# A two-layer decoder with a mixture of experts: expert weights in 16 KB runs, the first expert's rows gathered, the routing lists computed in one piece

## The reference, cut to what matters

```python
h = rms_norm(x, ffn_norm[layer])                  # 512 x 1024
grp_p = softmax(h @ w_group + b_group)            # 4 groups, the best one is taken
top_p, top_i = top_k(softmax(logits of that group), 2)   # 2 of its 4 experts
combine[token, expert] = weight of that expert for that token (0 for the other 14)
for e in range(16):
    act = silu(h @ w_gate[e]) * (h @ w_up[e])     # w_gate, w_up: 1024 x 512
    y = y + combine[:, e:e + 1] * (act @ w_down[e])      # w_down: 512 x 1024
x = x + y
```

## Time and profile before

| | us |
|---|---|
| median of 3 runs (lowest, highest) | 1287.82 (1285.38, 1289.57) |
| the profiled execution: its time | 1285.25 |
| the profiled execution: its span | 1283.5 |
| TensorE busy in the span | 1180.3 (92%) |
| VectorE busy | 914.7 (71%) |
| ScalarE busy | 674.1 (53%) |
| DMA, mean over the span | 220 GB/s |
| the two MoE parts | about 340 to 665 and 944 to 1283.5 |

### The profile page before, as it was taken

The page is one execution under the profiler, slowest core; times in us unless marked ns, Lnnn a source line. Parts: engine busy times, 40 slices in busy tenths (PEclk is TensorE's granted clock), DMA queues, the critical chain, the costliest instruction groups (busy, mean ns, idle before and its releaser), DMA issues.

```text
span 1283.5 us, 16959 instructions
## 1 busy us (share of the span) xinstructions
PE 1180.3 (92%) x5788; PEld 898.5 (70%) x5788; DVE 914.7 (71%) x1251; ACT 674.1 (53%) x843; POOL 97.3 (8%) x128
## 2 busy tenths in 40 slices
PE   5999879999799999999878999999979999999986
PEld 4776669878776766766646688887876666667663
DVE  4646668656579888888967247646558898888886
ACT  4335651134347778777733242132426777787862
POOL 1120000000010000000030000001001100000003
PEclk9999999999899999999989999999979999999998
DMA  6231110123599999999860240113169999999955
GB/s 221 91 89 66 66 66 1 66 73 125 187 331 363 366 385 390 384 382 384 332 220 1 70 136 15 66 66 131 66 257 303 368 381 381 383 391 385 381 203 209
DMA packets 129423, 281.75 MB, mean 220 GB/s; under 512 B 18945, under 2 KB 19457, under 8 KB 129361
## 3 DMA queue, kind: packets, MB, share of 16 engines
q1 hardware_dynamic: 119680, 246.98, 53.2%
q0 software_dynamic: 5888, 20.97, 5.3%
q10 hardware_dynamic: 3792, 12.98, 2.7%
HBM read 262.05 MB, written 18.87 MB: 219 GB/s over the span
## 4 chain that ended last, share of the span: by engine, by line
PE 57%; DVE 25%; issue 9%; ACT 6%; POOL 1%; DMA 1%; DVEq 1%; ACTq 0%; SPq 0%
PE PS L1109 16%; PE PS L1111 15%; PE PS L1110 15%; DVE expert_w_low L1824 10%; PE PS L1213 4%; DVE group_low L1612 2%; PE PS L1343 2%; ACT weight_high L870 1%; PE PS L1148 1%; DVE xgT_low L1832 1%; DVE act L1845 1%; DVE score_max L1743 1%; DVE G L1502 1%; PE PS L1323 1%; DVE hT_low L1596 1%
## 5 line engine op out<-in xcount | busy, mean ns | idle before, releaser
L1824 DVE TENSOR_TENSOR expert_w_low<-expert_w,weight_high 128x1024 fp32r<-128x1024 f32 x368 | 426.5, 1221 | 75.0 <-ACT weight_high L870 71.3
L870 ACT ACTIVATE weight_high<-expert_w 128x1024 fp32r<-128x1024 f32 x384 | 375.5, 1049 | 69.6 <-PE PS L1111 61.9
L1109 PE MATMUL PS<-weight_high,xgT_high 128*96 128x512 f32 x512 | 204.5, 399 | 2.6 <-DVEq L1834 2.6
L1111 PE MATMUL PS<-weight_high,xgT_low 128*96 128x512 f32 x512 | 203.2, 397 | 0.0
L1110 PE MATMUL PS<-expert_w_low,xgT_high 128*96 128x512 f32 x512 | 202.1, 395 | 0.0
L1109 PE MATMUL PS<-group_high,hT_high 128*128 128x512 f32 x416 | 172.2, 414 | 13.9 <-DVEq L1599 9.5
L1111 PE MATMUL PS<-group_high,hT_low 128*128 128x512 f32 x416 | 165.3, 397 | 0.0
L1110 PE MATMUL PS<-group_low,hT_high 128*128 128x512 f32 x416 | 165.0, 397 | 0.0
L1109 PE MATMUL PS<-weight_high,actT_high 128*96 128x512 f32 x256 | 104.3, 407 | 19.4 <-DVEq L1882 18.9
L1612 DVE TENSOR_TENSOR group_low<-group_w,group_high 128x1024 fp32r<-128x1024 f32 x68 | 80.8, 1223 | 43.4 <-ACT group_high L894 39.5
L1109 PEld LDWEIGHTS PS<-weight_high,xgT_high 128*96 128x96 f32 x512 | 83.3, 163 | 36.0 <-DVEq L1834 2.7
(11 more groups left out here) (251 smaller groups left out, 1469.9 us busy)
## 6 DMA issues: line engine op xcount, KB each, us to landing
expert_w<-in_moe_w_gate SPq DMA_DIRECT2D x32, 2048.0 KB, 13.7
expert_w<-in_moe_w_up SPq DMA_DIRECT2D x32, 2048.0 KB, 15.0
expert_w<-in_moe_w_down SPq DMA_DIRECT2D x32, 2048.0 KB, 13.5
group_w<-in_even_w_in SPq DMA_DIRECT2D x6, 2048.0 KB, 7.8
group_w<-in_odd_w_in SPq DMA_DIRECT2D x6, 2048.0 KB, 8.1
y_rows<-yb ACTq DMA_DIRECT2D x30, 384.0 KB, 6.1
group_w<-in_even_w_out SPq DMA_DIRECT2D x2, 2048.0 KB, 7.9
h_rows<-h SPq DMA_DIRECT2D x8, 512.0 KB, 11.3
```

Source lines behind the costliest of these rows:

```text
L870: act_(hi, w, ACT.Copy).then_inc(w_hi, 1)
L1109: pe.matmul(out, ah, bh, start=first, stop=False)
L1111: return pe.matmul(out, al, bh, start=False, stop=final)
L1824: tt(lo, w, hi.bitcast(F32), ALU.subtract).then_inc(w_lo, 1)
```

## The change

1. The weight view becomes `(p k) n -> p (a k) n`: partition p takes rows 8p to 8p+7 (gate, up) or 4p to 4p+3 (down), one run of 16 KB. To match, `h` ahead of the MoE is written with its columns in the order k, j from j*8+k, and `act` from j*4+k. VectorE does both by reading its two inputs with a step of 8 or of 4 elements; the output is written in order. The mixers' weights keep their view.
2. `oh0` and its 64 matmuls go. The rows of expert 0 are gathered like the others: the first indirect DMA takes column 0 of `idx`, the loop gathers 1 to 15, and TensorE transposes block 0's rows with `rows_T(0)`. SP no longer waits for the matmuls before it loads gate of expert 2.
3. VectorE's order at the start changes: after the one-hots `ohj` come two pieces of `first_low(1)`, `idx`, the other two pieces, the tokens' weights, the last expert's one-hots, the overflow counts, `b` and `j`, the instructions of `slots`, then the low part of block 0's rows, the instructions of `further`, the low part of block 1's rows, all of gate of expert 1, `times_up(0)`. ScalarE: rows 0, rows 1, the last one-hots' copy, high part of gate, then `silu(0)`. TensorE: gate 0, `rows_T(1)`, the last one-hots' transposes, up 0.

```diff
-                    src = t["moe_w_" + name][l, bass.ds(e, 1)].rearrange("a (k p) n -> p (a k) n", p=P)
+                    src = t["moe_w_" + name][l, bass.ds(e, 1)].rearrange("a (p k) n -> p (a k) n", p=P)
...
                 sp.wait_ge(h_stored, 16 * NT * (l + 1))
                 bk.wait_full(sp, ("route", l))
-                bk.wait_full(sp, ("xgT", l))
                 expert("gate", 2, 5)
...
-                pool.indirect_dma_start(xg[0:CAP, :], None, hbuf[l][:], bass.IndirectOffsetOnAxis(idx[:, 1:2], 0)
+                pool.indirect_dma_start(xg[0:CAP, :], None, hbuf[l][:], bass.IndirectOffsetOnAxis(idx[:, 0:1], 0)
                                         ).then_inc(gathered, 16)
-                with pool.Fori(2, NE) as b:
+                with pool.Fori(1, NE) as b:
...
                 rows_T(0, 0)
-                silu(0)
-                high(GATE, which=range(0, 2))
                 rows_T(1, 1)
-                high(GATE, which=range(2, SPLITS))
                 key = ("lastT", l)
                 bk.wait_full(sc, key)
                 link(act_(lastT[:], bank(key)[0:CAP], ACT.Copy))
                 sc.sem_inc(bk.freed(key), 1)
+                bk.wait_full(sc, ("gate", l))
+                high(GATE)
+                silu(0)
...
-                key = ("xgT", l)
-                pe.wait_ge(h_ready, NT * (2 * l + 2))
-                pe.wait_ge(oh0_ready, l + 1)
-                bk.acquire_in_loop(pe, key, 0)
-                for c in range(KD):
-                    for i in range(NT):
-                        ins = pe.matmul(PS[:, 4 + c // 4, c % 4 * CAP:(c % 4 + 1) * CAP], h[:, i, c * P:(c + 1) * P],
-                                        oh0[:, i], start=i == 0, stop=i == NT - 1)
-                ins.then_inc(bk.filled(key), 1)
...
+                rows_T(0)
                 pe.wait_ge(xgT_ready, l * NE + 1)
                 into("gate", 0, 0, 0, 0, 0)
-                into("up", 0, 0, 1, 0, 0, lambda: rows_T(1))
+                rows_T(1)
                 key = ("lastT", l)
...
+                into("up", 0, 0, 1, 0, 0)
                 expert_loop(pe, block_pe)
...
+            act_parts = act[0:CAP].rearrange("p (k j) -> p k j", k=DE // P)
+            def in_parts_of(a):
+                return a.rearrange("p (j k) -> p k j", k=DE // P)
...
-                        stt(h[:, i], x[:, i], xrs[:, i:i + 1], normw[:], ALU.mult, ALU.mult).then_inc(h_ready, 1)
+                        dst, xi, nw = h[:, i], x[:, i], normw[:]
+                        if n % 2:
+                            dst = dst.rearrange("p (k j) -> p k j", k=KD)
+                            xi, nw = (a.rearrange("p (j k) -> p k j", k=KD) for a in (xi, nw))
+                        stt(dst, xi, xrs[:, i:i + 1], nw, ALU.mult, ALU.mult).then_inc(h_ready, 1)
...
-                for i in range(NT):
-                    ins = ts(oh0[:, i], iota_f[:, 0:CAP], rank[:, i, 0:1], r["M"][:, i, 0:1], ALU.is_equal, ALU.mult)
-                link(ins)
-                ve.sem_inc(oh0_ready, 1)
...
+                first_low(1, range(0, 2))
+                key = ("idx", l)
+                bk.wait_full(ve, key)
+                link(cp(idx[:, 0:NE], bank(key)[0:CAP, 0:NE]))
+                ve.sem_inc(idx_ready, 1)
+                ve.sem_inc(bk.freed(key), 1)
+                first_low(1, range(2, SPLITS))
...
-                    link(tt(act[0:CAP], bank(("up", l))[0:CAP], ex[0:CAP], ALU.mult))
+                    link(tt(act_parts, in_parts_of(bank(("up", l))[0:CAP]), in_parts_of(ex[0:CAP]), ALU.mult))
...
-                    if is_int and b == 0:
-                        slots()
-                    if is_int and b == NE - 3:
-                        further()
```

More of the change, by code:

```diff
@@ L368, in build @@
         ).items():
-            if name == "ein":
-                oh0 = at("first_onehot", [P, NT, CAP], F32, cursor[0])
             rt[name] = sb("r_" + name, [P] + shape)
@@ L418, in build @@
         idxcol_ready, gathered = sem("idxcol_ready"), sem("gathered")
-        oh0_ready = sem("first_onehot_ready")
         xgT_ready, ex_ready = sem("xgT_ready"), sem("gate_silu_ready")
@@ L798, in _ @@
                 pool.sem_inc(gather_issued, 1)
-                pool.indirect_dma_start(xg[0:CAP, :], None, hbuf[l][:], bass.IndirectOffsetOnAxis(idx[:, 1:2], 0)
+                pool.indirect_dma_start(xg[0:CAP, :], None, hbuf[l][:], bass.IndirectOffsetOnAxis(idx[:, 0:1], 0)
                                         ).then_inc(gathered, 16)
-                with pool.Fori(2, NE) as b:
+                with pool.Fori(1, NE) as b:
                     bk.wait_full(pool, ("xgT", l), b - 1)
-                    gather(l, b, idxcol_ready, b + (l * (NE - 2) - 1), gathered)
+                    gather(l, b, idxcol_ready, b + l * (NE - 1), gathered)
                 pool.wait_ge(eid_ready, l + 1)
@@ L864, in _, with high @@
             for l in range(NL):
-                def high(p0, b=0, par=0, which=range(SPLITS)):
+                def high(p0, b=0, par=0):
                     wait_loaded(sc, l, p0, b, par)
-                    for part in which:
+                    for part in range(SPLITS):
                         w, hi, _ = parts(l, p0, par, part)
@@ L1364, in rows_T @@
                     key = ("xgT", l)
-                    pe.wait_ge(gathered, b * 16 + 16 * l * (NE - 1))
+                    pe.wait_ge(gathered, b * 16 + 16 * (l * NE + 1))
                     bk.acquire_in_loop(pe, key, b)
@@ L1908, in _ @@
                 link(tt(r["w_last"], r["w_of"][:, 0], r["w_of"][:, 1], ALU.add))
+                for i in range(NT):
+                    ins = ts(ohj[:, i], iota_f[:, 0:CAP], rank[:, i, NE - 1:NE], r["M"][:, i, NE - 1:NE], ALU.is_equal, ALU.mult)
+                link(ins)
+                ve.sem_inc(last_ready, 1)
                 link(ts(r["nx"], total, float(CAP), None, ALU.is_gt))
@@ L1913, in _ @@
                 link(tt(r["off"], r["off"], r["nx"], ALU.subtract))
[L1914 to L1920, removed]
                 link(ts(r["q"], rank, float(CAP), None, ALU.is_ge))
@@ L1930, in _ @@
                 link(stt(r["j"], r["q"], -float(CAP), rank, ALU.mult, ALU.add))
[L1931 to L1936, removed]
+                for of, by in (("bc", "b"), ("jc", "j")):
+                    link(tt(r["tA"], r["OH"], r[by].unsqueeze(1).broadcast_to(both), ALU.mult))
+                    link(red(r[of], r["tA"], AX, ALU.add))
+                link(stt(r["jz"], r["bc"], float(NE - 1), r["jc"], ALU.not_equal, ALU.mult))
+                link(stt(r["sl"], r["bc"], float(CAP), r["jz"], ALU.mult, ALU.add))
+                link(cp(slot[:], r["sl"]))
+                rows_T(0, 0)
+                it8 = iota_f[:, 0:16].unsqueeze(2).broadcast_to([P, 16, NE])
+                off8 = r["off"].unsqueeze(1).broadcast_to([P, 16, NE])
+                nx8 = r["nx"].unsqueeze(1).broadcast_to([P, 16, NE])
+                link(tt(r["ein"], it8, off8, ALU.subtract))
+                link(tt(r["ein2"], r["ein"], nx8, ALU.is_lt))
+                link(stt(r["ein2"], r["ein"], 0.0, r["ein2"], ALU.is_ge, ALU.mult))
+                link(tt(r["ein2"], r["ein2"], iota_f[:, 0:NE].unsqueeze(1).broadcast_to([P, 16, NE]), ALU.mult))
+                link(red(r["eidf"], r["ein2"], AX, ALU.add))
+                link(red(r["eidf"][:, 15:16], r["nx"], AX, ALU.add))
+                link(cp(eid[:], r["eidf"]))
+                ve.sem_inc(eid_ready, 1)
                 rows_T(1, 1)
-                low(GATE, which=range(2, SPLITS))
+                low(GATE)
                 times_up(0)
@@ L1952, in _ @@
                         ve.wait_ge(ov_pe[l], b * 4 + 3)
-                        tt(act[0:CAP], PS[0:CAP, 1, :], ex[0:CAP], ALU.mult).then_inc(ov_ve[l], 1)
+                        tt(act_parts, in_parts_of(PS[0:CAP, 1, :]), in_parts_of(ex[0:CAP]), ALU.mult).then_inc(ov_ve[l], 1)
             for kind, i in sums[NL - 1]:
```

## The result

The changed kernel took **1304.78 us** (median of 3 runs, 1303.42 to 1305.05) against 1287.82: slower by 1.3%, ratio 1.0131 with a 95% interval of 1.0102 to 1.0159. The forecast was 1292.3 with a range to 1301. Its profiled span is 1301.7 us against 1283.5, so 18.2 us are to be found.

What follows compares the result with a forecast made beforehand. TensorE's matmuls were taken to bound the blocks, VectorE right behind. Per layer 3.3 + 0.74 + 3.8 + 0.5 + 0.4 - 1.6 - 4.9 = +2.2 us, twice +4.5: 1292.3 us on the median, 8-in-10 range 1283.5 to 1301.

Steps and rivals of the forecast that it cites:

- The start: From `r_R` to the first gate matmul: 17.75 us instead of 13.96, set by VectorE's list, +3.8 us a layer.
- the gather comes late: Rival at the start: gather rows wait behind 16 KB runs, +4.2 to +6 us in all, 1296.5 to 1298.3; chance 0.10.
- Stepped reads: VectorE's `act` and `h`: 0.72 ns an element, 0.37 us per `act` on 9 of 16 blocks, 0.74 us for `h`.
- Both rivals on the steps: At `act` and `h`: steps cost nothing, 1284.2 us, chance 0.22; or two stepped inputs add up, 1300.4 us, chance 0.18.
- the lower bound of 0: VectorE's stepped reads: least extra cost 0, since L1692's second level, step of 2, takes the plain 693 ns.
- The runs themselves: Expert weight loads in 16 KB runs: 0 us, since nothing waits for a load.
- Block 0: ScalarE's `silu(0)` and table load after high part of gate delay VectorE's low of down: +0.4 us a layer, bounds 0 and +0.9.
- What goes: `slots` out of block 1, -1.6 us; `further` out of block 14 with its low clock, -4.9 us together, a layer.
- The clock: Low clock around 640 us goes, saving 1.7 us; gate matmuls at the start run low 4 us instead of 3, +0.5.

Runs made afterwards that it cites:

- the lists moved alone: Kernel before with b, j and slots moved into VectorE's pause beside the one-hot matmuls and further taking the place of b and j: 1275.43 us, ratio 0.9896.

## Why the prediction was wrong

**The start: this step failed.** "So the gather hides with 0.4 us to spare" took the median landing of 7.2 us from the old blocks. The parts beside it were right, or nearly: `idx` at 4.72, the issue at 5.86 (forecast 5.87), the list done at 16.1; only the handover behind it was 0.11 us instead of 0.66, so the list alone gives a start of 17.2 (measured with all loads held) and not 17.75. The gather was at the edge even with short runs: 8.0 us to TensorE in L0, 8.8 in L1, where it ended the start. In the changed kernel it took 12.2 and 11.8 us, so the start took 21.65 and 21.18 instead of 17.75: 7.3 us over the forecast in all. The rival "the gather comes late" named the place and the mechanism, 6 rows an engine each behind a 16 KB run, which is what the packet counts show, but had 0.10 and was priced by the worst landing of the old runs. I argued against it that the blocks show 7.2 "under the same load"; that row was measured with 2 and 4 KB runs, which the change takes away. And SP's earlier load of gate of expert 2 was booked at 0 "as nobody waits for it". Holding it back gives 7.3 us: it put nobody off but the gather, which by then TensorE waits for.

**Stepped reads: right.** +0.39 us an `act` against 0.37: runs and steps alone cost 3.0 and 3.5 us a layer between first gate matmul and the last `act`, 8 and 9 times 0.39 (forecast 3.3 for 9), 8.7 in all (forecast for `act` and `h` 8.1). `h` costs 0.91 against 0.74. Both rivals on the steps fall. The figure of 2.50 ns a column by the Trainium skill, page "Vector Engine (DVE) Microarchitecture Reference", section "Measured stream behaviour on trn2", is for a longer step; here two stepped inputs took 1072 / 512 = 2.09 ns, of which the steps added 0.77. The same table has 1.76 ns for two sources that hop 4 KiB at every element, 0.71 over its contiguous row, which is nearer.

One row was read wrongly, with no harm to the sum. The row of L1692 in the earlier trace rows, `Q<-Q,decay`, holds only the levels that read runs of two and more adjacent elements. The second level, single elements with a step of 2, is `Q<-Q,C`:

```profile
200.65 0.69 DVE L1692 TENSOR_TENSOR Q<-Q,C 128x512 f32<-128x512 f32 x1 [0.32 <-DVE AT L1708]
```

It takes the same 0.69 us, so the lower bound of 0 stands. But that the page's rule, full rate only in runs of two or more adjacent words, "agrees with both rows" is true of the rows as printed and not of this one: a step of 2 on single words costs nothing here.

**The runs themselves: half right.** No load is waited for, and the loads land sooner (gate 12.2 us, was 13.7). But beside 16 KB runs the median gather lands 3.3 us later, which the blocks cover and the start does not.

**Block 0: right in size, wrong in place.** `act` of expert 0 to that of expert 1 went from 17.62 to 18.46 us: +0.84, forecast 0.37 and 0.4. The two do not add up as I had them: with the steps alone the stretch takes 18.01 us, with the new order alone (no runs, no steps) 18.42, with both 18.46, so on top of the new order the step of `act` adds only 0.04 us. I had put the order's price on low of down; it came as a wait for the PSUM bank, and low of down was next in line.

**What goes: right.** With the lists moved alone it is 6.3 and 6.2 us a layer, forecast 6.5. In after `act` of expert 14 to that of 15 takes 18.42 us, was 22.42: -4.0, where the forecast, with one step, had -4.5.

**The clock: right at 640 us, too small at the start.** The low stretch at 640 us went, as said. In after down of expert 15 has one at 665 us and takes 8.91 us to the next layer's matmuls (665.08 to 673.99) instead of 7.34 (655.93 to 663.27). That is no new loss: before had a low stretch at 665 us as well, on the matmuls behind down. The first two lines are before (window, then TensorE's timeline), the third is after:

```profile
665.00:670.00 5.00, 3.64 (x5) 1.01 (x3) 3.63 (x4) 2.51 (x4) 0.58 (x1) 0.67 0.41 164
663.27 5.37 PE L1122 MATMUL PS<-y_last,last_onehot_T 96*128 96x512 f32 x8 [1.55 <-ACTq L1054]
673.99 3.67 PE L1118 MATMUL PS<-y_last,last_onehot_T 96*128 96x512 f32 x8 [1.55 <-ACTq L1050]
```

Down and these eight together take 12.71 us before and 12.58 in after, so the 1.7 us saved at 640 are kept. Layer 1 has the same pair of low stretches. In the kernel with only the lists moved, layer 0 has no low stretch here (down from 653.78 to 661.13, then 3.67 us) and layer 1 has one on down. What the clock forecast missed is the start: the gate matmuls ran low for 4.5 us (clock 0.50 up to 376.0 us), where I took 4, and the first gate matmul to `act` of expert 0 took 0.95 and 0.78 us more than before, where I had 0.5. In the kernel without runs and steps they ran low for 5.8 us in layer 0, and it is 1.57 and 1.45 us more.

**Left over.** The spans differ by 18.2 us, and the forecast had 4.5. The start has 7.3 of the rest, the blocks 2.8 (the -2.3 a layer came as -1.25 and -0.57), and the stretches outside 3.7. Of the 3.7, 0.7 are the steps of the two `act` of expert 15, which I had counted in the blocks (TensorE's down starts 0.36 and 0.35 us later behind them), 0.3 are `h`, and 1.1 lie at the end of the program, where TensorE waits 1.16 us for VectorE, which had waited 2.26 us for a gather of results. The 1.4 up to the first `r_R` are open. They may be chance: the kernel before and the one with only the lists moved have the same instructions up to there and reach it at 347.63 and 351.96 us. Of the blocks' 2.8, which are 3.5 with those steps of `act` taken out, 0.7 are the clock at the start and 1.1 the two blocks 14; the rest is open.

## What to carry to other kernels

A landing time holds only for the transfers that were beside it: before a small scattered gather goes on the critical path, ask how long the runs are that share its DMA engines, and which loads your own change issues just ahead of it. Here, by the packet counts, every row waited for one run, so the price was about the rows of an engine times the time of a run. A load that nobody waits for can still be in the way. And look first whether the work to be moved fits a pause that is already there: here the pause next to the one-hot matmuls took it all, and those matmuls were what paid for the pause.

## What was not expected of the hardware

Contiguous 16 KB runs cut the packets from 129423 to 60013 and the weight loads' landing by 1.5 us, and raised the median landing of the gathers of 96 rows from 7.2 to 10.5 or 10.8 us at the same 387 GB/s; the stores of `y_rows` went from 6.1 to 8.5 us. A gather with nothing beside it took 4.5 us from issue to TensorE. Beside the loads its packets and theirs passed in about equal numbers, with 16 KB packets (48 to 49) as with 2 KB ones (100 to 119).
